# Neighbouring expert tables: one gathered 8 KB row for each pick instead of two of 4 KB, with weights in pairs

## The chip, the cores and the metric

The kernel runs on one core of a Trainium2 chip. The metric is device time in microseconds from start to end of one execution; the median of several is compared. The engines are TensorE (PE, matrix products into PSUM), VectorE (DVE), ScalarE (ACT), GpSimd (POOL, here almost only the issuer of indirect DMAs) and SyncE (SP, the issuer of all other DMAs). Each engine runs its own instructions in program order and waits on semaphores.

## The reference, cut to what matters

Two transformer blocks on 256 tokens of width 1024, all in float32. The first has neighbourhood attention, a convolution and a 16-expert feed-forward layer. The second has differential attention with a spatial gating branch and then, as its feed-forward layer, PEER: for each token and each of 8 heads 16 of 16384 experts are picked, and each expert is one row of `u_tab` and one of `v_tab`.

```python
def peer(h, w_query, sub_keys, u_tab, v_tab):
    xt = h.reshape(T, D)                                   # T = 256, D = 1024
    q = rmsnorm((xt @ w_query).reshape(T, PEER_HEADS, 2, PEER_PK_DIM))
    s = jnp.einsum('thpd,pnd->thpn', q, sub_keys).astype(jnp.float32)
    s1, i1 = lax.top_k(s[:, :, 0], PEER_TOPK)
    s2, i2 = lax.top_k(s[:, :, 1], PEER_TOPK)
    ...
    best, pos = lax.top_k(cand, PEER_TOPK)
    eidx = jnp.take_along_axis(cidx, pos, axis=-1)
    gate = jax.nn.softmax(best, axis=-1)

    def one(args):
        xb, ib, gb = args
        act = jax.nn.gelu(jnp.einsum('td,thkd->thk', xb, u_tab[ib]), approximate=False) * gb.astype(xb.dtype)
        return jnp.einsum('thk,thkd->td', act, v_tab[ib])
```

The lookup moves 256 x 8 x 16 rows of 4 KB from each table, 268 MB in all, against 527 MB for everything else.

## The kernel before, in words

The tokens stand on the 128 partitions in two halves, a = 0 and 1. `work` lists the 16 pairs (half, head); its index is `ix`. For each `ix` there are 16 picks k = 0 to 15, so a pick has the number n = 16 ix + k, 0 to 255. One pick handles one expert for each of the 128 tokens.

A pick goes through these steps:

- Routing: `rt0` to `rt4` (scores on TensorE, top 16 and indices `EI[:, ix, :]` on VectorE, roots and exponentials on ScalarE). GpSimd's gathers of `ix` wait for its indices (event `ei`).
- u: GpSimd gathers 128 rows of `peer_u_2` into a 4 KB buffer (in each partition), line 1636; VectorE takes the dot with the token's vector `HB`, line 1304, into `DOT[:, ix, k]`. The u buffer is then free.
- Weights, once for each `ix` after k = 15: GELU on ScalarE (line 1595), then on VectorE the product with the gate (`weights`, line 1312), which gives `WT`.
- v: GpSimd gathers 128 rows of `peer_v_2`; ScalarE writes `ident` scaled by the weight of each token into one of 4 diagonals `DI` (line 1602); TensorE multiplies diagonal and row, two instructions of `v_step` (line 790) that run as four matmuls of 128x512, and accumulates in two PSUM banks through all 128 picks of a half. The v buffer is free when the matmuls are done.

The order of all of it is one list, `ORDER`, made by `mixer_order`; each engine goes through it and does what is its own. In the PEER part the list has u(ix, k) and v(ix-1, k) side by side, so v is 16 picks behind u. Mixed in are the routing steps of the next `ix`, one at each odd k, and what is left of the second block's mixer for the other half and its queries (`late`, one item at each n that is a multiple of 3). `more_a` and `more_q` are no work: they mark where attention buffers and query weights are done with, and so where the row buffers get more room. `more_a` stands after n = 72 and `more_q` after n = 144, before as after the change. `take` gives the banks of a half to the sums, `leave` ends a half (norm, gain, residual, store).

`row_places` gives the buffers in rotation: 8 for u while ix = 0; then, from `share` on, 4 for u and 4 for v; 6 and 6 from `more_a` on, 10 and 10 from `more_q` on. A gather waits until the last user of its buffer is done.

Weights come by SyncE in blocks of 2 MB; in the PEER part these are `w_branch_attn` and `w_out` (stages `ba`, `op`) and `peer_w_query` (`qm`).

## Time and profile before

| | us |
|---|---|
| median of 3 executions | 2317.37 |
| lowest and highest | 2315.95, 2331.9 |
| the profiled execution, its own time | 2325.88 |
| its span, first to last instruction | 2323.9 |
| busy in the span: TensorE, VectorE, GpSimd, ScalarE | 1756.5, 740.3, 567.2, 392.1 |
| mean granted TensorE clock | 0.893 of full |
| DMA bytes and mean rate | 796.88 MB, 343 GB/s |

The times of single instructions come from the one profiled execution. Its span has 40 slices of 58 us in the strips of the page. GpSimd's first gather starts at 1526.75 us, and its last at 2300.51 us; so the lookup takes the last third of the time, and its first half runs beside the rest of the mixer. DMA share is the mean busy share of 16 DMA engines; it can show 1.00 at quite different GB/s.

### The profile page before, as it was taken

Reading aid. Unit: us, or ns where it says so; the run is one execution under the profiler, and the core shown is the slowest. Engines: PE = TensorE matmul, PEld = TensorE weight load, DVE = VectorE, ACT = ScalarE, POOL = GpSimd, SP = SyncE. Lnnn points to the kernel's source line nnn. Section 1 sums busy time; section 2 is a strip of 40 time slices with the busy share of each in tenths; the row PEclk is TensorE's granted clock in tenths of the full one; section 3 lists DMA queues with packets and bytes.
Section 4 is the critical chain, followed back from the end, with each engine's and each line's share of the span. In section 5 each row is a group of like instructions: output and inputs, shape, how many; then the busy total and the mean of one; then the engine's idle time right before and its main releaser. Section 6 shows DMA issues by size and latency. Waiting matters only on the chain.

```text
span 2323.9 us, 18524 instructions
## 1 busy us (share of the span) xinstructions
PE 1756.5 (76%) x7200; PEld 764.3 (33%) x7200; DVE 740.3 (32%) x1869; ACT 392.1 (17%) x836; POOL 567.2 (24%) x521
## 2 busy tenths in 40 slices
PE   8999656776765566666669999767778888766677
PEld 7656111331211111111124454463333445322223
DVE  5723001000000000000032131366675764766552
ACT  1411010000000000000011442233322222222211
POOL 0000000000000000000000000047676666777774
PEclk9987888887888878787789999889999999999999
DMA  9647999999999999999954332569999999999997
GB/s 370 215 172 298 413 427 427 423 424 424 424 428 428 428 428 428 428 427 428 427 191 160 134 138 79 190 238 365 320 379 388 405 373 359 375 369 369 355 373 292
DMA packets 159334, 796.88 MB, mean 343 GB/s; under 512 B 12304, under 2 KB 12432, under 8 KB 134160
## 3 DMA queue, kind: packets, MB, share of 16 engines
q1 hardware_dynamic: 85520, 527.24, 55.7%
q0 software_dynamic: 73728, 268.47, 30.6%
q8 instruction: 58, 0.95, 0.2%
q14 instruction: 28, 0.23, 0.0%
HBM read 794.61 MB, written 1.05 MB: 342 GB/s over the span
## 4 chain that ended last, share of the span: by engine, by line
PE 40%; DMA 40%; DVE 7%; POOL 7%; ACT 3%; issue 3%; DVEq 0%; POOLq 0%; ACTq 0%
DMA AR<-in_w_down 18%; DMA AR<-in_w_up 15%; PE PS L373 13%; PE PS L790 10%; POOL AR L1636 7%; DMA AR<-in_peer_v,AR 6%; PE PS L594 3%; PE PS L753 2%; PE PS L612 2%; PE PS L384 2%; PE PS L486 1%; DVE AR L856 1%; DMA AR<-in_peer_u,AR 1%; DVE AR L858 1%; PE PS L624 1%
## 5 line engine op out<-in xcount | busy, mean ns | idle before, releaser
L1636 POOL DMA_INDIRECT AR<-in_peer_u,AR x256 | 282.7, 1104 | 1458.4 <-DVE AR L1295 1357.5
L790 PE MATMUL PS<-AR 128*128 128x512 f32 x1024 | 506.9, 635 | 162.2 <-DMA AR<-in_peer_v,AR 93.3
L594 PE MATMUL PS<-AR 128*32 128x512 f32 x2048 | 310.4, 743 | 191.1 <-DMA AR<-in_w_up 127.0
L1304 DVE CUSTOM_DVE_ANT_0 AR<-AR 128x1024 f32<-128x1024 f32 x256 | 308.4, 1221 | 172.8 <-DMA AR<-in_peer_u,AR 172.8
L790 PEld LDWEIGHTS PS<-AR 128*128 128x128 f32 x1024 | 190.3, 199 | 451.2 <-issue 314.0
L373 PE MATMUL PS<-AR 128*128 128x512 f32 x736 | 327.5, 600 | 8.7 <-DVE AR L831 7.9
L1636 POOL DMA_INDIRECT AR<-in_peer_v,AR x256 | 282.7, 1104 | 108.3 <-PE PS L790 56.0
L612 PE MATMUL PS<-AR 128*32 128x512 f32 x1024 | 172.1, 807 | 108.5 <-DMA AR<-in_w_down 99.7
L1035 DVE TENSOR_TENSOR AR<-AR,PS 128x512 f32<-128x512 f32 x16 | 11.0, 688 | 609.5 <-PE PS L594 609.5
L594 PEld LDWEIGHTS PS<-AR 128*32 128x32 f32 x2048 | 63.8, 123 | 424.9 <-DMA AR<-in_w_up 204.4
L373 PEld LDWEIGHTS PS<-AR 128*128 128x128 f32 x736 | 139.2, 193 | 176.1 <-issue 173.1
L1602 ACT ACTIVATE AR<-PK,AR 128x128 f32<-128x128 f32 x256 | 90.7, 393 | 155.0 <-PE PS L790 144.0
L612 PEld LDWEIGHTS PS<-AR 128*32 128x32 f32 x1024 | 32.5, 130 | 231.4 <-DMA AR<-in_w_down 156.9
L1043 DVE COPY AR<-PS 128x512 f32<-128x512 f32 x16 | 11.1, 691 | 286.0 <-PE PS L612 286.0
L384 PE MATMUL PS<-AR 128*128 128x256 f32 x384 | 83.4, 379 | 0.9 <-DVE AR L826 0.9
L624 PE MATMUL PS<-AR 128*128 128x512 f32 x128 | 66.3, 665 | 14.4 <-DVE AR L1043 14.4
L384 PEld LDWEIGHTS PS<-AR 128*128 128x128 f32 x384 | 72.9, 190 | 12.0 <-issue 2.2
L1444 ACT ACTIVATE AR<-PS 128x512 f32<-128x512 f32 x16 | 9.6, 597 | 398.0 <-PE PS L594 398.0
L753 PE MATMUL PS<-AR 128*128 128x128 f32 x512 | 65.6, 291 | 2.1 <-DVE AR L831 2.1
L753 PEld LDWEIGHTS PS<-AR 128*128 128x128 f32 x512 | 64.0, 206 | 4.8 <-DVE AR L826 2.5
L1448 ACT COPY AR<-PS 128x512 f32<-128x512 f32 x16 | 9.4, 585 | 319.9 <-PE PS L601 319.9
L624 PEld LDWEIGHTS PS<-AR 128*128 128x128 f32 x128 | 25.9, 213 | 62.1 <-issue 62.1
(251 smaller groups left out, 1209.3 us busy)
## 6 DMA issues: line engine op xcount, KB each, us to landing
AR<-in_w_gate SPq DMA_DIRECT2D x64, 2048.0 KB, 26.2
AR<-in_w_up SPq DMA_DIRECT2D x64, 2048.0 KB, 25.8
AR<-in_w_down SPq DMA_DIRECT2D x64, 2048.0 KB, 26.4
AR<-in_w_in SPq DMA_DIRECT2D x23, 2048.0 KB, 10.1
AR<-in_w_ada SPq DMA_DIRECT2D x12, 2048.0 KB, 10.0
AR<-in_peer_w_query SPq DMA_DIRECT2D x8, 2048.0 KB, 17.3
AR<-in_w_out SPq DMA_DIRECT2D x6, 2048.0 KB, 13.3
AR<-in_w_branch_attn SPq DMA_DIRECT2D x4, 2048.0 KB, 10.5
```

The costliest lines, as they stand in the source:

```text
L373: i = pe.matmul(PS[:, b, :], src[:, j, a * 128:(a + 1) * 128], IN[key][:, j, :], start=(j == 0), stop=(j == 7))
L384: i = pe.matmul(PS[:, b, q * 256:(q + 1) * 256], IN[key][:, j, (e + q) * 128:(e + q + 1) * 128], src[:, j, :], start=(j == 0), stop=(j == 7))
L486: x = pe.matmul(PS[:, b, :], MT[:, 4 * q + j, a * 128:(a + 1) * 128], IN[key][:, j, n * 512:(n + 1) * 512], start=(j == 0), stop=(j == 3))
L594: x = pe.matmul(PS[32 * q:32 * q + 32, bk, :], XS[:, j, e * 32:(e + 1) * 32], IN[key][:, jj, q * 512:(q + 1) * 512], start=(j == 0), stop= ...
L612: x = pe.matmul(PS[32 * g:32 * g + 32, b, :], HDT[:, s, fq * 32:(fq + 1) * 32], IN[key][:, s, dc * 512:(dc + 1) * 512], start=(fq == 0 and ...
L624: x = pe.matmul(PS[:, y, :], GE[:, r, dc, a * 128:(a + 1) * 128], EO[:, r, :], start=(e == 0), stop=(e == 15), skip_group_check=True)
L753: x = pe.matmul(PS[:, b, q * 128:(q + 1) * 128], IN[key][:, j, (2 * r + q) * 128:(2 * r + q + 1) * 128], HT[:, j, a * 128:(a + 1) * 128], ...
L790: x = pe.matmul(PS[:, ACC[a][m], :], DI[:, n % 4, :], AR[:, off + m * 512:off + (m + 1) * 512], start=(h == 0 and k == 0), stop=(h == 7 an ...
L856: w.step(v.scalar_tensor_tensor(DW[:, j, :], UP[:, j, k:k + 256], c, DW[:, j, :], MULT, ADD))
L1304: v.tensor_tensor_reduce(rows, rows, HB[:, a, :], 1.0, 0.0, MULT, ADD, DOT[:, ix, k:k + 1]).then_inc(*w.hit("dot", ix, k))
L1602: act.activation(DI[:, n % 4, :], ident, ACT.Copy, scale=WT[:, ix, k:k + 1]).then_inc(*w.hit("diag", n))
L1636: pool.indirect_dma_start(out=AR[:, off:off + 1024], out_offset=None, in_=D["peer_u_2" if key == "u" else "peer_v_2"], in_offset=bass.Indi ...
```

## The change

The host puts the two tables side by side, `peer_uv_2` with rows of 8 KB, u first. One gather for each pick brings both, into a buffer of 8 KB for each partition: 128 pieces of 8 KB instead of 256 of 4 KB. The dot reads the first half, the matmuls the second, and the buffer is free when the matmuls are done.

The order list has one loop over n. After row n, for even n, come the weights of the pair (n-2, n-1) and the v steps of these two; GELU of a pair stands after its odd row. So v is 2 picks behind u instead of 16, and GELU (ScalarE) and the product with the gate (VectorE) are 128 instructions each on 2 columns instead of 16 on 16 columns. The buffers are 4 of 8 KB, 7 from `more_a` on (one more place is used, at `W0 + 2048`), 11 from `more_q` on.

```diff
--- before.py
+++ after.py
@@ -294,26 +294,25 @@
                 todo += x
             todo += [("rt1", 0), ("rt2", 0), ("rt3", 0), ("rt4", 0)]
             routes = []
-            for ix in range(17):
-                if ix == 1:
-                    todo.append(("share",))
-                if ix == 8:
+            for n in range(257):
+                ix, k = divmod(n, 16)
+                if n == 128:
                     todo.append(("take", 1))
-                for k in range(16):
-                    if ix < 16:
-                        todo.append(("u", ix, k))
-                    if ix >= 1:
-                        todo.append(("v", ix - 1, k))
-                    if (16 * ix + k) % 3 == 0 and late:
-                        todo += late.pop(0)
-                    if k == 0 and ix < 15:
-                        routes += [(f"rt{s}", ix + 1) for s in range(5)]
-                    if (k % 2 or ix == 0) and routes:
-                        todo.append(routes.pop(0))
-                if ix < 16:
-                    todo.append(("wts", ix))
-                if ix in (8, 16):
-                    todo.append(("leave", ix // 8 - 1))
+                if n < 256:
+                    todo.append(("row", ix, k))
+                if n and n % 2 == 0:
+                    todo.append(("wts", *divmod(n // 2 - 1, 8)))
+                    todo += [("v", *divmod(j, 16)) for j in (n - 2, n - 1)]
+                if n in (128, 256):
+                    todo.append(("leave", n // 128 - 1))
+                if n % 3 == 0 and late:
+                    todo += late.pop(0)
+                if k == 0 and ix < 15:
+                    routes += [(f"rt{s}", ix + 1) for s in range(5)]
+                if (k % 2 or ix == 0) and routes:
+                    todo.append(routes.pop(0))
+                if k % 2:
+                    todo.append(("gelu", ix, k // 2))
             assert not late and not routes
             return todo
 
@@ -321,28 +320,29 @@
         ROWS = {}
 
         def row_places():
             def slot(i):
-                return [NARENA + i * SLOT + 1024 * k for k in range(4)]
-
-            bufs, n = {"u": slot(4) + slot(5), "v": []}, {"u": 0, "v": 0}
-            free = {x: ("used", "wq", 1, 0) if x >= NARENA + 5 * SLOT else ("used", "wq", 0, 0) for x in bufs["u"]}
-            for u, *x in ORDER:
-                if u == "share":
-                    bufs["v"], bufs["u"], n["u"] = bufs["u"][4:], bufs["u"][:4], 0
-                if u in ("more_a", "more_q"):
-                    new = {"u": [o + 16384, o + 18944], "v": [o + 17408, o + 19968]} if u == "more_a" else {"u": slot(2), "v": slot(3)}
-                    for key in "uv":
-                        bufs[key] += new[key]
-                        for k in new[key]:
-                            free[k] = ("mm", "av", 15) if u == "more_a" else ("used", "wq", 2 if key == "u" else 3, 1)
-                if u in ("u", "v"):
-                    k = bufs[u][n[u] % len(bufs[u])]
-                    n[u] = (n[u] + 1) % len(bufs[u])
-                    ROWS[(u, *x)] = k, free[k]
-                    free[k] = ("dot", *x) if u == "u" else ("mm", "row", *x)
+                return [NARENA + i * SLOT, NARENA + i * SLOT + 2048]
+
+            bufs, n = slot(4) + slot(5), 0
+            free = {k: ("used", "wq", i // 2, 0) for i, k in enumerate(bufs)}
+            for stage, *x in ORDER:
+                if stage == "more_a":
+                    new = [o + 16384, o + 18944, W0 + 2048]
+                    free.update({k: ("mm", "av", 15) for k in new})
+                    bufs = bufs[:n] + new + bufs[n:]
+                if stage == "more_q":
+                    new = slot(2) + slot(3)
+                    free.update({k: ("used", "wq", 2 + i // 2, 1) for i, k in enumerate(new)})
+                    bufs = bufs[:n] + new + bufs[n:]
+                if stage == "row":
+                    k = bufs[n]
+                    n = (n + 1) % len(bufs)
+                    ROWS[(*x,)] = k, free[k]
+                    free[k] = ("mm", "row", *x)
 
         row_places()
 
@@ -783,11 +783,11 @@
             def v_step(ix, k):
                 a, h = work[ix]
                 n = 16 * ix + k
-                off, _ = ROWS["v", ix, k]
+                off, _ = ROWS[ix, k]
                 w.wait_ge("diag", n)
-                w.wait_ge("rowv", ix, k)
+                w.wait_ge("landed", ix, k)
                 for m in range(2):
-                    x = pe.matmul(PS[:, ACC[a][m], :], DI[:, n % 4, :], AR[:, off + m * 512:off + (m + 1) * 512],
+                    x = pe.matmul(PS[:, ACC[a][m], :], DI[:, n % 4, :], AR[:, off + 1024 + m * 512:off + 1024 + (m + 1) * 512],
                                   start=(h == 0 and k == 0), stop=(h == 7 and k == 15), skip_group_check=True)
                 x.then_inc(*w.hit("mm", "row", ix, k))
 
@@ -1295,21 +1295,22 @@
                 v.tensor_copy(EI[:, ix, :], EF[:, 0:16]).then_inc(*w.hit("ei", ix))
                 v.tensor_scalar(SMX[:, ix, 0:1], BV[:, ix, 0:1], -1.0, None, MULT).then_inc(*w.hit("smx", ix))
 
-            def u_step(ix, k):
+            def row(ix, k):
                 a, h = work[ix]
-                off, _ = ROWS["u", ix, k]
+                off, _ = ROWS[ix, k]
                 rows = AR[:, off:off + 1024]
-                w.wait_ge("rowu", ix, k)
+                w.wait_ge("landed", ix, k)
                 w.wait_ge("hb", a, 1)
                 v.tensor_tensor_reduce(rows, rows, HB[:, a, :], 1.0, 0.0, MULT, ADD, DOT[:, ix, k:k + 1]).then_inc(*w.hit("dot", ix, k))
 
-            def weights(ix):
-                sm = SMX[:, ix, :]
-                w.wait_ge("gate", ix)
-                w.step(v.reciprocal(sm[:, 1:2], sm[:, 1:2]))
-                w.wait_ge("gelu", ix)
-                w.wait_step()
-                v.scalar_tensor_tensor(WT[:, ix, :], GT[:, ix, :], sm[:, 1:2], WT[:, ix, :], MULT, MULT).then_inc(*w.hit("wt", ix))
+            def weights(ix, p):
+                sm, two = SMX[:, ix, :], slice(2 * p, 2 * p + 2)
+                if p == 0:
+                    w.wait_ge("gate", ix)
+                    w.step(v.reciprocal(sm[:, 1:2], sm[:, 1:2]))
+                    w.wait_step()
+                w.wait_ge("gelu", ix, p)
+                v.scalar_tensor_tensor(WT[:, ix, two], GT[:, ix, two], sm[:, 1:2], WT[:, ix, two], MULT, MULT).then_inc(*w.hit("wt", ix, p))
 
             def leave(a):
                 ps = PS[:, ACC[a][0]:ACC[a][1] + 1, :].rearrange("p b n -> p (b n)")
@@ -1326,7 +1327,7 @@
                     "cmb": att_combine, "gain1": lambda: row_of("g1", G1, COL[:, 3, :]), "gain2": lambda: row_of("g2", G2, COL[:, 4, :]),
                     "hn1": hn1, "hn2": hn2, "ht": heads_turn, "bae": bae, "ope": ope, "up1": up1, "up2": up2, "fn1": fn1, "fn2": fn2,
                     "norm_turn": lambda a: scaled("h3", HT[:, :, a * 128:(a + 1) * 128], a, COL[:, 0, :], COL[:, 5, :]),
-                    "ft": ffn_turn, "rt0": rt0, "rt1": rt1, "rt2": rt2, "rt3": rt3, "rt4": rt4, "u": u_step, "wts": weights, "leave": leave}
+                    "ft": ffn_turn, "rt0": rt0, "rt1": rt1, "rt2": rt2, "rt3": rt3, "rt4": rt4, "row": row, "wts": weights, "leave": leave}
             for stage, *x in ORDER:
                 if stage in mine:
                     mine[stage](*x)
@@ -1590,13 +1591,14 @@
                     act.copy(d[:, 4 * q:4 * q + 4, :], PS[:, banks.at("hb", a, q), :].rearrange("p (j q) -> p j q", j=4)).then_inc(
                         *w.hit("hb", a, q))
 
-            def weights(ix):
-                w.wait_ge("dot", ix, 15)
-                act.activation(WT[:, ix, :], DOT[:, ix, :], ACT.Gelu).then_inc(*w.hit("gelu", ix))
+            def gelu(ix, p):
+                two = slice(2 * p, 2 * p + 2)
+                w.wait_ge("dot", ix, 2 * p + 1)
+                act.activation(WT[:, ix, two], DOT[:, ix, two], ACT.Gelu).then_inc(*w.hit("gelu", ix, p))
 
             def v_step(ix, k):
                 n = 16 * ix + k
-                w.wait_ge("wt", ix)
+                w.wait_ge("wt", ix, k // 2)
                 if n > 3:
                     w.wait_ge("mm", "row", *divmod(n - 4, 16))
                 act.activation(DI[:, n % 4, :], ident, ACT.Copy, scale=WT[:, ix, k:k + 1]).then_inc(*w.hit("diag", n))
@@ -1613,7 +1615,7 @@
                     "hn1": lambda a: root(("on", a), SSO[:, a * 8:a * 8 + 8]), "yt": lambda a: copied("yt", YT, a), "ope": ope,
                     "up1": lambda a: root(("y2", a), ss5[:, a:a + 1]), "up2": up2, "fn1": lambda a: root(("x5", a), ss6[:, a:a + 1]),
                     "qm": qm, "qs": qs, "rt0": lambda ix: root(("q", ix), RQ[:, work[ix][0], 2 * work[ix][1]:2 * work[ix][1] + 2]),
-                    "rt4": rt4, "back": back, "wts": weights, "v": v_step, "leave": leave}
+                    "rt4": rt4, "back": back, "gelu": gelu, "v": v_step, "leave": leave}
             for stage, *x in ORDER:
                 if stage in mine:
                     mine[stage](*x)
@@ -1629,17 +1631,17 @@
             w.step(pool.memset(msk[0:64, 0:1], 1.0))
             pool.memset(msk[64:128, 1:2], 1.0).then_inc(*w.hit("msk"))
 
-            def gather(key, ix, k):
-                off, free = ROWS[key, ix, k]
+            def row(ix, k):
+                off, free = ROWS[ix, k]
                 w.wait_ge("ei", ix)
                 w.wait_ge(*free)
-                pool.indirect_dma_start(out=AR[:, off:off + 1024], out_offset=None, in_=D["peer_u_2" if key == "u" else "peer_v_2"],
+                pool.indirect_dma_start(out=AR[:, off:off + 2048], out_offset=None, in_=D["peer_uv_2"],
                                         in_offset=bass.IndirectOffsetOnAxis(ap=EI[:, ix, k:k + 1], axis=0)).then_inc(
-                    *w.hit(f"row{off}", key, ix, k, also=[("row" + key, ix, k)], by=16))
+                    *w.hit(f"row{off}", ix, k, also=[("landed", ix, k)], by=16))
 
             for stage, *x in ORDER:
-                if stage in ("u", "v"):
-                    gather(stage, *x)
+                if stage == "row":
+                    row(*x)
 
 
 
@@ -1834,8 +1836,9 @@
     for n in ("w_gate", "w_up", "w_down"):
         arrays[n] = g[n][0]
     arrays["final_g"] = g["final_g"]
-    for n in ("w_in_2", "w_branch_attn_2", "w_branch_sgu_2", "w_out_2", "peer_w_query_2", "peer_u_2", "peer_v_2", "b_gate_2"):
+    for n in ("w_in_2", "w_branch_attn_2", "w_branch_sgu_2", "w_out_2", "peer_w_query_2", "b_gate_2"):
         arrays[n] = g[n][0]
+    arrays["peer_uv_2"] = np.concatenate([g["peer_u_2"][0], g["peer_v_2"][0]], 1)
     arrays["rows"] = np.stack([g["sgu_ln_g_2"][0], g["sgu_ln_b_2"][0]])
     return {k: np.ascontiguousarray(a) for k, a in arrays.items()}
 
```

## Rows read from the trace of the kernel before

**Rows 1.** The page, part 2: TensorE's clock and DMA share in 40 slices.

```profile
PEclk9987888887888878787789999889999999999999
DMA  9647999999999999999954332569999999999997
```

**Rows 2.** The stages as windows, busy us (instructions), clock, DMA share, GB/s.

```profile
core 0: us, PE busy (x) PEld busy (x) DVE busy (x) ACT busy (x) POOL busy (x), PEclk, DMA share, GB/s
1526.70:1732.00 205.30, 153.19 (x543) 80.62 (x542) 139.58 (x375) 65.78 (x164) 145.18 (x129) 0.90 0.93 343
1732.00:1964.50 232.50, 200.29 (x688) 106.57 (x687) 145.04 (x382) 54.66 (x131) 156.33 (x144) 0.96 1.00 381
1964.50:2287.00 322.50, 233.43 (x497) 87.59 (x495) 199.62 (x505) 72.63 (x167) 252.79 (x229) 0.97 0.98 371
```

**Rows 3.** The timeline of GpSimd (start, duration, both us): u 72 and u 144.

```profile
1731.97 0.94 POOL L1636 DMA_INDIRECT AR<-in_peer_u,AR  x1 [0.30 <-issue]
...
1964.54 0.94 POOL L1636 DMA_INDIRECT AR<-in_peer_u,AR  x1 [0.30 <-issue]
```

**Rows 4.** Two more windows: an expert stretch, and the last gathers.

```profile
700.00:1150.00 450.00, 275.59 (x1557) 60.53 (x1556) 14.18 (x28) 8.88 (x15) 0.00 (x0) 0.80 1.01 428
2261.00:2300.00 39.00, 32.42 (x70) 12.59 (x71) 13.07 (x24) 7.22 (x19) 29.57 (x31) 1.00 1.03 410
```

**Rows 5.** Groups of instructions from 1480 us on (busy us, mean ns | idle before).

```profile
L1636 POOL DMA_INDIRECT AR<-in_peer_u,AR x256 | 282.7, 1104 | 1458.4 <-DVE AR L1295 1357.5 <-issue 74.4 <-DVE AR L1304 26.6
...
L1595 ACT ACT_TABLE_LOAD x15 | 19.2, 1283 | 0.3
```

**Rows 6.** Line 1636, GpSimd's gathers, 1964.5 to 2287: idle before (us, times).

```profile
  issue: 54.3, 178
  PE PS L790: 15.7, 51
```

**Rows 7.** The timeline: GELU, product of weights and the scaled copies after the last dot.

```profile
2287.00 0.21 ACT L1595 ACTIVATE AR<-AR 128x16 f32<-128x16 f32 x1 [7.72 <-DVE AR L1304]
...
2287.25 0.23 DVE L1312 SCALAR_TENSOR_TENSOR AR<-AR 128x16 f32<-128x16 f32 x1 [0.21 <-ACT AR L1595]
2287.52 0.69 ACT L1602 ACTIVATE AR<-PK,AR 128x128 f32<-128x128 f32 x2 [0.30 <-DVE AR L1312]
```

**Rows 8.** The timeline: the first gather, the first dot, a gather among dots.

```profile
1526.75 1.08 POOL L1636 DMA_INDIRECT AR<-in_peer_u,AR  x1 [1357.48 <-DVE AR L1295]
...
1531.27 1.22 DVE L1304 CUSTOM_DVE_ANT_0 AR<-AR 128x1024 f32<-128x1024 f32 x1 [4.74 <-DMA AR<-in_peer_u,AR]
...
1559.93 1.99 POOL L1636 DMA_INDIRECT AR<-in_peer_u,AR  x1 [0.30 <-issue]
```

**Rows 9.** The timeline: scaled copy to matmul, and matmul to gather.

```profile
1661.11 0.98 ACT L1602 ACTIVATE AR<-PK,AR 128x128 f32<-128x128 f32 x3
1661.57 0.30 PEld L790 LDWEIGHTS PS<-AR 128*128 128x128 f32 x2 [0.27 <-ACT AR L1602]
...
2150.62 1.96 PE L790 MATMUL PS<-AR 128*128 128x512 f32 x4 [0.59 <-DMA AR<-in_peer_v,AR]
...
2152.82 1.01 POOL L1636 DMA_INDIRECT AR<-in_peer_v,AR  x1 [0.31 <-PE PS L790]
```

**Rows 10.** The timeline: four matmuls after an idle time.

```profile
1655.45 3.49 PE L790 MATMUL PS<-AR 128*128 128x512 f32 x4 [2.48 <-ACT AR L1602]
```

**Rows 11.** DMA from issue to landing of the gathers, stage A; stage B with its bytes.

```profile
DMA to landing us min/median/max: 4.5/6.4/10.1
...
DMA to landing us min/median/max: 5.0/8.4/13.0
...
DMA packets 27061, 88.50 MB, mean 381 GB/s; under 512 B 2408, under 2 KB 2408, under 8 KB 27049
```

**Rows 12.** The chain that ended last: a block of 16 matmuls.

```profile
1752.91 6.87 PE PS L373 x16
```

**Rows 13.** The timeline: the last matmuls, 17 picks.

```profile
2287.13 29.42 PE L790 MATMUL PS<-AR 128*128 128x512 f32 x68 [0.60 <-DMA AR<-in_peer_v,AR]
```


## The prediction

> **What bounds the kernel now.** I read the 40 slices first [rows 1]: the digits change character in slice 27, where GpSimd begins to work and the DMA share climbs back to 9. That is the expert lookup (PEER), and only there does the change act. Then the same stretch cut at the picks at which the buffers grow [rows 2]. I number the 256 picks n = 16·ix + k. The order list gives `more_a` right after row 72 and `more_q` right after row 144. The gathers of u 72 and u 144 are the 129th and the 273rd on GpSimd's queue, and they start at 1731.97 and 1964.54 us [rows 3]. So there are three stages: A, 1526.7 to 1732 (72 picks, 205 us, few buffers), B, 1732 to 1964.5 (72 picks, 232.5 us), C, from there to the last product at 2316.6 (112 picks).
>
> In stage C the DMA share is 0.98, but at 371 GB/s. That isn't this core's ceiling: the experts' weights ran at 428 GB/s in slices that show 1.01, and the gathers themselves at 410 GB/s at the end of the stage [rows 4]. What sets C is GpSimd's issue. A gather costs 1104 ns there [rows 5], and 0.30 us of idle time "issue" follows it: of 229 gathers 178 waited for nothing else, and for buffers only 15.7 us in all [rows 6]. (1.104 + 0.30) x 2 = 2.81 us a pick, and 114 picks a 322.5 us stage is 2.82. TensorE (233 of 322.5 us), VectorE (200) and ScalarE (73) have room. Stage B is crowded: TensorE 200 of 232.5 us, DMA share 1.00 with w_query and w_out loads beside the rows. Stage A has slack everywhere (TensorE 153, VectorE 140 of 205 us) and still takes about 2.85 us a pick.
>
> **The change, part by part.**
>
> *One gather for two.* It removes 256 instructions of GpSimd, 256 x 1.41 = 361 us of its queue. Stage C then loses its bound. The next one is the transfer: 1.049 MB a pick at 428 GB/s is 2.45 us, at 410 GB/s 2.56 us; I take 2.50, as the 8 KB pieces lie between the 4 KB of the gathers and the longer ones of the weights. TensorE needs 1.96 us a pick at most, VectorE about 200/114 = 1.75. GpSimd's 1.41 is hidden under the transfer; uncovered it would be late only if an issue took over 2.5 us.
>
> *Weights in pairs.* ScalarE gets 112 more GELUs of 0.21 us (24 us), VectorE 112 more products of 0.23 us (26 us) [rows 7]. Also, a GELU now stands between the root and the exponential of a head, so up to 16 more table loads of 1.28 us (20 us) [rows 5]. All lie in time that both engines wait for rows (ScalarE is busy for 66 of 205 us in the fullest stage); only the one product that releases each pair is on a path, and I count it below. Without that cover they would cost 70 us.
>
> *Buffers.* This is the part that decides. Before, a u buffer was free once its dot was done and a v buffer was filled only 16 picks later, shortly before its product. Now one 8 KB buffer is held from the issue until both matmuls are done. There are 4 of them until row 72, 7 until row 144, then 11; before it was 4 + 4, 6 + 6, 10 + 10. And there is a new wait: on VectorE `wts` of the pair (n-2, n-1) is queued behind `row` n, which waits for row n to land. Behind it wait the copies of `ident` scaled by the weights (the diagonals), the matmuls of n-2, and the gather of n+2, which needs that buffer. With 4 buffers this is a closed loop for each two picks, with nothing of it overlapped:
> - gather issued to dot started, 4.52 us for 512 KB on an empty queue [rows 8], plus the other 512 KB, 1.22 us at 428 GB/s: 5.74
> - dot of row n: 1.22, then 0.05 (an estimate; both are on VectorE) to the product of weights, 0.23, and 0.04 to ScalarE [rows 7, 8]: 1.54
> - diagonal started to matmul started: 0.45 (1661.11 to 1661.57) [rows 9]
> - four matmuls 1.96, and 0.24 until GpSimd starts the next gather [rows 9]: 2.20
>
> Together 9.93 us for two picks, where two gathers' worth of issue allowed 5.6. To that I add two terms. The clock: stage A had 0.90 of full clock with TensorE busy for 75%; in the loop it is busy for about half. After 2.5 us of idle time the four matmuls took 3.49 us [rows 10] instead of 1.96, the lower of the two clock levels (1.2 for 2.4 GHz); bounds 0 and 1.53. The expert stage, with TensorE busy for 61%, has a mean of 0.80 [rows 4]; with less work I take half of the turns at the lower level, 0.75. Late mixer work and routing mixed in between: before, 112 gathers from 1559.93 to 1731.97 [rows 3, 8] took 3.07 us a pick where the issue alone gives 2.81, 0.26 a pick or 0.5 a pair; the bounds are 0 and 1.5 (routing instructions on VectorE are short and lie in the 6 us in which it waits for a row). So 11.2 us a pair, with bounds 9.9 and 13.
>
> Row 4 needs the product of row 0, behind the dot of row 2: row 2 lands at 1526.75 + 5.7 + 2 x 2.45 = 1537.4, and 3.95 us of chain and 0.24 of issue later gather 4 goes out at 1541.6. Gather 72 follows 34 pairs later: 1541.6 + 34 x 11.2 = 1922.4, against 1732.0. Stage A costs +190 us.
>
> *A queue effect inside the loop.* GpSimd's gathers take 0.94 us when VectorE is not in a dot, and up to 1.99 when dots run back to back, as at 1559.93 [rows 8]. Gather n+2 goes out when the dots are over, so I take 0.94 (it is inside the 5.74), and 1.05 x 34 = 36 us as the upper end. The Trainium skill, SBUF — State Buffer, Who interferes with whom, says that a VectorE instruction with two SBUF inputs contends with a GpSimd instruction that reads SBUF, and that the second to start waits; the rows above agree, and by it alone the price would be anything from 0 to those 36 us.
>
> *Stage B.* With 7 buffers the same loop turns 5 picks at a time: 9.9/5 = 2.0 us, under the 3.23 a pick that the stage took. TensorE's work and the bytes are what they were, so I leave it at 232.6 us. Lower bound: 88.5 MB [rows 11] at 410 GB/s, 216 us. Upper: one 6.87 us block like those of `op` or `ba` [rows 12] in each turn, 18.1/5 = 3.6 a pick, 260 us. Gather 144 at 2155.0.
>
> *Stage C.* 11 buffers give 9 picks a turn, 1.1 us: the transfers rule. Row 144 lands some 9 us after its issue (8.4 us was the median for 512 KB in the crowded stage) [rows 11], at 2164. Then 111 x 2.50 = 277.5: row 255 lands at 2441.5. The indices of the next head are ready after dot 16·ix + 9 and 3.5 us of `rt4`, with six rows still in flight, so that isn't late.
>
> *The end.* Before, 68 matmuls of the last 17 picks stood behind the last dot (29.4 us [rows 13]). Now it is dot 1.22, GELU 0.3, product 0.27, diagonal 0.49, two picks 1.96 + 1.72: 6.0 us, to 2447.5, and the same 7.35 us of `leave`, from 2316.6 to the end of the span. Span 2454.9 against 2323.9: +131 us. The profiled execution took 2325.88, 2 us more than its span, and lies 8.5 us over the median; the difference goes on the median: 2317.4 + 131 = 2448.
>
> In brief: stage A +190, stage B 0, stage C and the end -59.
>
> **The rivals.**
> (1) *Faster: the number of transfers is what counts.* If the loop of stage A weren't closed, because rows landed early enough that four buffers cover them, A would stay at 205 us and only the -59 remain: 2258 us. For it: GpSimd's issue is the plain bound in C. Against it: it decides at a loop of 11.2 - 131/34 = 7.35 us, and landing plus dot alone are 6.96. The Trainium skill, DMA: Bandwidth & Descriptors, Bandwidth, asks for transfers of at least 1 MiB; by it this change is right, and the time would be this rival's. The landing of stage A (4.5 us at best, 6.4 in the median [rows 11]) neither proves nor refutes it.
> (2) *The loop is longer.* Late work falls into it, and in stage B too: 13 us a pair (+61) and 3.6 us a pick in B (+27): 2536 us. For it: in-order queues, where a scaled copy waits behind an exponential that waits for VectorE. Against it: 6 us of idle time in each turn.
> (3) *The 8 KB row isn't one piece.* If the gather writes it as two, an issue costs 2 x 0.94 us: +0.94 in each turn (32 us), and the transfer stays at 2.56 us (+7): 2487 us. No row of before has an 8 KB gather.
>
> **How the numbers follow.** My forecast with its own bounds (loop 9.9 to 12.5, B 216 to 245, C 2.45 to 2.6) runs from 2380 to 2515 and gets 0.72; rival 2 0.11, rival 3 0.08, rival 1 0.06, nothing measurable 0.03. The range 2375 to 2530 takes in rival 3 and the near half of rival 2. A difference under 1% can hardly be told from none here. Faster 0.06, same 0.03, slower 0.91.
>
> **What would show it.** Right: GpSimd idle in stage A for some 10 us at every second gather, ended by the matmuls; gathers in pairs; DMA share near half and TensorE's clock below 0.9 until `more_a`; stage A near 395 us; stage C at 2.5 us a pick with TensorE or VectorE waiting for rows; a last block of matmuls of two picks. Wrong: a gather 72 before 1880, a landing of 8 KB rows much under 5.7 us, or stage C still at 2.8 us. It would all fall if the loop had overlap that I missed, above all if VectorE could take a pair's weights ahead of the next row.

## The result, and the profile after

The changed kernel takes 2505.7 us (median of 4, 2502.39 to 2512.94), the kernel before 2322.72 in the same comparison: ratio 1.0785, 95% interval 1.0759 to 1.0811. The profiled execution took 2506.88 us with a span of 2505.1.

Page, part 2, of the changed kernel: clock and DMA share in 40 slices of 63 us.

```profile
PEclk9988878888888778877999998777777889999999
DMA  9657999999999999998443246555555988899997
```

In slices 25 to 31 the DMA share stays at 5 and 6, where the kernel before was at 9 from its slice 28 on [rows 1], and in slices 26 to 31 the clock is at 7. From slice 32 on the DMA share is at 8 and 9. The same in windows, cut where GpSimd issues the first gather and rows 72 and 144 (columns as in rows 2):

```profile
core 0: us, PE busy (x) PEld busy (x) DVE busy (x) ACT busy (x) POOL busy (x), PEclk, DMA share, GB/s
1528.60:1937.10 408.50, 235.45 (x612) 113.98 (x612) 153.95 (x428) 97.28 (x224) 68.68 (x72) 0.77 0.54 195
1937.10:2206.10 269.00, 207.53 (x653) 107.82 (x652) 144.10 (x394) 73.96 (x173) 78.32 (x73) 0.90 0.86 326
2206.10:2473.00 266.90, 214.93 (x486) 90.85 (x486) 193.92 (x533) 83.81 (x208) 130.70 (x111) 0.94 1.01 421
```

| stage (start of issue to start of issue, us) | before | forecast | after |
|---|---|---|---|
| first gather | 1526.8 | 1526.8 | 1528.6 |
| A, to row 72 | 205.2 | 395.6 | 408.5 |
| B, to row 144 | 232.6 | 232.6 | 268.9 |
| C with the end, to the end of the span | 359.4 | 299.9 | 299.0 |

The loss is in A (+203) and B (+36); C with the end gives back 60. The next lines are those of line 1638, GpSimd's gathers in stage A of the changed kernel: number and durations; the idle time before them by what ended it (us, times); who waited for them (us, times); and the time from issue to landing.

```profile
L1638 POOL DMA_INDIRECT AR<-in_peer_uv,AR x72: 933/936/1375, 1528.6 to 1928.2; - x72
...
  PE PS L790: 330.3, 68
...
  DVE AR L1304: 226.6, 66
...
DMA to landing us min/median/max: 5.3/5.7/9.7
```

GpSimd stood 330 of 408 us at a matmul, 68 of 72 times, and VectorE 227 us at a landing. Neither is overlapped with the other, as one turn of the loop shows (timeline of the changed kernel: start, duration, both us):

```profile
1800.40 0.94 POOL L1638 DMA_INDIRECT AR<-in_peer_uv,AR  x1 [8.29 <-PE PS L790]
...
1806.53 1.23 DVE L1304 CUSTOM_DVE_ANT_0 AR<-AR 128x1024 f32<-128x1024 f32 x1 [8.32 <-DMA AR<-in_peer_uv,AR]
...
1807.68 0.22 DVE L1313 SCALAR_TENSOR_TENSOR AR<-AR 128x2 f32<-128x2 f32 x1
1807.93 0.69 ACT L1604 ACTIVATE AR<-PK,AR 128x128 f32<-128x128 f32 x2 [9.49 <-DVE AR L1313]
...
1808.38 6.45 PE L790 MATMUL PS<-AR 128*128 128x512 f32 x8 [6.65 <-ACT AR L1604]
...
1812.44 0.94 POOL L1638 DMA_INDIRECT AR<-in_peer_uv,AR  x1 [9.49 <-PE PS L790]
```

The gather of an even row goes out at 1800.40 (that of the odd row 1.6 us behind it isn't shown). The dot starts 6.13 us later, the pair's weights come right behind the dot, then the scaled copies and the first four matmuls, and at 1812.44 the next gather: 12.04 us for two picks. The mean turn from gather 4 to gather 72 is (1937.15 - 1548.44)/34 = 11.43 us.

Two groups of the page, for comparison with rows 5 (busy us, mean ns | idle before):

```profile
L1638 POOL DMA_INDIRECT AR<-in_peer_uv,AR x256 | 278.6, 1088 | 2024.0 <-DVE AR L1295 1385.7
...
L1597 ACT ACT_TABLE_LOAD x37 | 47.5, 1283 | 0.7
```

A gather of 8 KB rows costs GpSimd what one of 4 KB did (1088 against 1104 ns), and there are 37 table loads at GELU's line instead of 15. The roots and exponentials beside it also load more often; in this part of the kernel there are 80 loads in all where there were 52. At the end of the kernel the last block of matmuls is four picks, not 17 [rows 13]:

```profile
2490.63 7.13 PE L790 MATMUL PS<-AR 128*128 128x512 f32 x16 [1.25 <-ACT AR L1604]
```

### The profile page after: what moved, and what is told of

The parts are those of the page before. It is cut to its first block, busy times and chain, and to the rows that moved or that the text cites. A ratio compares the mean times of both kernels' runs of the same rounds, so it can differ in the third digit from the quotient of the medians.

```text
span 2505.1 us, 18590 instructions
## 1 busy us (share of the span) xinstructions
PE 1825.0 (73%) x7200; PEld 799.6 (32%) x7200; DVE 758.4 (30%) x1981; ACT 452.0 (18%) x976; POOL 280.4 (11%) x265
## 3 DMA queue, kind: packets, MB, share of 16 engines
HBM read 794.61 MB, written 1.05 MB: 318 GB/s over the span
## 4 chain that ended last, share of the span: by engine, by line
DMA 43%; PE 40%; DVE 10%; ACT 4%; issue 2%; POOL 1%; DVEq 0%; POOLq 0%; ACTq 0%
DMA AR<-in_w_down 16%; DMA AR<-in_w_up 14%; DMA AR<-in_peer_uv,AR 13%; PE PS L373 12%; PE PS L790 12%; DVE AR L1304 3%; PE PS L594 2%; PE PS L753 2%; PE PS L612 2%; PE PS L384 2%; PE PS L486 1%; DVE AR L856 1%; ACT AR L1604 1%; DVE AR L858 1%; PE PS L624 1%
## 5 line engine op out<-in xcount | busy, mean ns | idle before, releaser
L790 PE MATMUL PS<-AR 128*128 128x512 f32 x1024 | 571.7, 714 | 290.5 <-ACT AR L1604 290.4
L1638 POOL DMA_INDIRECT AR<-in_peer_uv,AR x256 | 278.6, 1088 | 2024.0 <-DVE AR L1295 1385.7
L790 PEld LDWEIGHTS PS<-AR 128*128 128x128 f32 x1024 | 225.6, 229 | 607.8 <-ACT AR L1604 348.6
L373 PE MATMUL PS<-AR 128*128 128x512 f32 x736 | 327.3, 600 | 8.7 <-DVE AR L831 7.9
L373 PEld LDWEIGHTS PS<-AR 128*128 128x128 f32 x736 | 139.0, 192 | 176.0 <-issue 173.1
L624 PE MATMUL PS<-AR 128*128 128x512 f32 x128 | 68.4, 683 | 14.4 <-DVE AR L1043 14.4
L384 PEld LDWEIGHTS PS<-AR 128*128 128x128 f32 x384 | 74.4, 194 | 12.6 <-issue 2.2
L753 PEld LDWEIGHTS PS<-AR 128*128 128x128 f32 x512 | 61.4, 199 | 5.6 <-issue 3.1
L1313 DVE SCALAR_TENSOR_TENSOR AR<-AR 128x2 f32<-128x2 f32 x128 | 28.0, 218 | 66.2 <-ACT AR L1597 65.9
L1597 ACT ACT_TABLE_LOAD x37 | 47.5, 1283 | 0.7
```

The lines of the kernel that those rows point to most:

```text
L373: i = pe.matmul(PS[:, b, :], src[:, j, a * 128:(a + 1) * 128], IN[key][:, j, :], start=(j == 0), stop=(j == 7))
L384: i = pe.matmul(PS[:, b, q * 256:(q + 1) * 256], IN[key][:, j, (e + q) * 128:(e + q + 1) * 128], src[:, j, :], start=(j == 0), stop=(j == 7))
L624: x = pe.matmul(PS[:, y, :], GE[:, r, dc, a * 128:(a + 1) * 128], EO[:, r, :], start=(e == 0), stop=(e == 15), skip_group_check=True)
L753: x = pe.matmul(PS[:, b, q * 128:(q + 1) * 128], IN[key][:, j, (2 * r + q) * 128:(2 * r + q + 1) * 128], HT[:, j, a * 128:(a + 1) * 128], ...
L790: x = pe.matmul(PS[:, ACC[a][m], :], DI[:, n % 4, :], AR[:, off + 1024 + m * 512:off + 1024 + (m + 1) * 512], start=(h == 0 and k == 0), s ...
L1313: v.scalar_tensor_tensor(WT[:, ix, two], GT[:, ix, two], sm[:, 1:2], WT[:, ix, two], MULT, MULT).then_inc(*w.hit("wt", ix, p))
```

## The experiments

The times of both kernels and of e1, e2, e5 and e9 are medians, those of the other runs single executions. Beside each stands the kernel before on the same chip. The first two lines of the table are the two kernels.

Stages A and B run to the issue of row (or u) 72 and 144, in one profiled execution of each run. Where two kernels do the same work, these stages agree closely: A is 329.8 in e1 and 331.5 us in e6, and 408.5 in the changed kernel and 408.6 in e3. Only B of the kernel before (232.6) and of e9 (227.7) are 5 us apart, so differences under some 5 us say little.

| run | edit | time, before beside it (us) | A | B |
|---|---|---|---|---|
| before | | 2322.7 | 205 | 233 |
| changed | | 2505.7, 2322.7 | 408.5 | 269 |
| e1 | changed, weights ahead of row | 2427.9, 2324.6 | 330 | 271 |
| e2 | changed, two tables | 2438.2, 2324.6 | 306 | 271 |
| e3 | changed, 4 buffers in B too | 2663.9, 2324.6 | 408.6 | 427 |
| e4 | changed, extra matmuls in A | 2507.4, 2324.6 | 403 | 270 |
| e5 | before, weights in pairs | 2339.6, 2318.0 | 210 | 239 |
| e6 | e1, v one step later | 2418.3, 2318.0 | 331.5 | 260 |
| e7 | e1, copy for GELU | 2394.4, 2318.0 | 309 | 258 |
| e8 | e5 with v 2 behind u | 2355.0, 2322.7 | 238 | 252.5 |
| e10 | e5 with v 6 behind u | 2365.8, 2322.7 | 232 | 257 |
| e11 | e8, v gathered with u | 2434.4, 2316.6 | 307.5 | 275 |
| e9 | before to row 143, then joined | 2296.6, 2318.0 | 206 | 228 |

Theory 1 was the closed loop of the prediction: with four buffers each turn holds two picks, and nothing in it overlaps. Its rivals: theory 2, slow 8 KB gathers; theory 3, the pairs with their table loads; theory 4, stage B bound by late work; and theory 5, formed after the first four runs, the short lag of v (2 picks behind u, not 16).

**e1, the queue place of the weights.**

```diff
-                if n < 256:
-                    todo.append(("row", ix, k))
                 if n and n % 2 == 0:
                     todo.append(("wts", *divmod(n // 2 - 1, 8)))
+                if n < 256:
+                    todo.append(("row", ix, k))
+                if n and n % 2 == 0:
                     todo += [("v", *divmod(j, 16)) for j in (n - 2, n - 1)]
```

> VectorE takes the weights of the pair (n-2, n-1) ahead of row n instead of behind it; everything else as changed. Theory 1 (the loop of stage A is closed by that queue place: landing of row n, dot, weights, diagonal, matmuls, next gather, for two picks): the loop then spans four picks: second gather 2.2 us after the first, landing 5.7, dot 1.2, GELU 0.3, weights and diagonal 0.75, matmuls 2.0 to 3.5, 0.24, so 12.2 to 13.7 us for four picks; stage A falls from 408 to 220 to 250 us, stage B from 269 to 235 to 260, the total to 2320 to 2360. Theory 2 (8 KB gathers into four buffers are slow whatever the order: landing and clock): stage A stays over 380 us and the total over 2470.

Measured: ratio to before 1.0453 (1.0423 to 1.0482); stages A and B of e1 in windows:

```profile
1523.30:1853.10 329.80, 202.56 (x613) 102.44 (x612) 154.47 (x428) 97.62 (x224) 75.04 (x73) 0.81 0.65 242
1853.10:2124.50 271.40, 205.54 (x653) 106.85 (x652) 143.44 (x391) 74.11 (x173) 76.63 (x73) 0.89 0.85 324
```

One list entry moved gives back 79 of the 203 us of stage A, so the place of `wts` behind `row` is a cause, and theory 2, as it was put, falls. But both are far outside what I expected: stage A is 80 us above the top of its range, the total 68, and B didn't move. Something takes the place of the wait that was removed. A part of it is VectorE's wait for GELU. The group of the product of a pair's weights in stage A, first in the changed kernel and then in e1 (busy us, mean ns | idle before):

```profile
L1313 DVE SCALAR_TENSOR_TENSOR AR<-AR 128x2 f32<-128x2 f32 x35 | 7.6, 217 | 1.1 <-ACT AR L1597 1.0
...
L1314 DVE SCALAR_TENSOR_TENSOR AR<-AR 128x2 f32<-128x2 f32 x35 | 7.7, 221 | 39.1 <-ACT AR L1598 39.1
```

Behind the dot of row n the GELU had long been done; ahead of it VectorE stands 39 us for ScalarE, with the dot of row n queued behind.

**e2, two tables.** Orders, pairs and buffer places are those of the changed kernel, but u and v are gathered by themselves, v right behind u on GpSimd, and u's half of the buffer is free after its dot.

```diff
-                w.wait_ge(*free)
-                pool.indirect_dma_start(out=AR[:, off:off + 2048], ..., in_=D["peer_uv_2"],
+                for key, at, free in (("u", off, free_u), ("v", off + 1024, free_v)):
+                    w.wait_ge(*free)
+                    pool.indirect_dma_start(out=AR[:, at:at + 1024], ..., in_=D["peer_u_2" if key == "u" else "peer_v_2"],
```

> Weights in pairs and v two picks behind u as changed, but two tables and two 4 KB gathers for each pick, u's buffer free after its dot, as many buffers of each as the changed kernel has of 8 KB. Theory 1 (u and v held together is half of the closed loop): the gather of u n no longer waits for matmuls of pick n-4 except through GpSimd's queue; M(n-4) to M(n) is three issues 3.96, landing 5.5, dot 1.2, 0.8, matmuls 2.0 to 3.5, so 13.5 to 15 us for four picks, stage A 240 to 270 us; stage C goes back to GpSimd's 2.8 us a pick (315 us); total 2340 to 2390. Theory 3 (the pairs with their table loads and the short lag cost by themselves): stage A stays near 400 us and the total is over 2500.

Measured: ratio 1.05 (1.0468 to 1.0531), stage A 306.4, B 271.0. Joining the rows, with all else equal, makes 2505.7 us of 2438.2: it costs 102 us in A and gives back 28 in C with the end (299.0 against 326.6). From row 144 to the last issue it gives back 42 (266.9 against 308.6), but 14 of these are lost again, as with the joined rows the end takes 32 us from the last issue and with two tables 18. Theory 3 alone doesn't hold, and theory 1 missed too: 306 is above its 240 to 270, and the total above its 2340 to 2390.

**e3, four buffers in stage B.**

```diff
                 if stage == "more_a":
                     ...
-                    bufs = bufs[:n] + new + bufs[n:]
+                    held = new
```

> The three buffers of more_a come into use only at more_q, so that four buffers last to row 144. Theory 1 (4-buffer loop of 11.4 us for two picks): stage B turns at the pace of stage A, 72 x 5.7 = 410 us against 269, total about 2645. Theory 4 (stage B is bound by TensorE's late blocks and the weights' loads, not by the loop): stage B under 320 us, total under 2560.

Stage B of e3, in a window:

```profile
1935.70:2362.30 426.60, 263.48 (x698) 129.96 (x697) 152.25 (x403) 76.67 (x183) 67.91 (x72) 0.79 0.57 208
```

Stage B takes 426.6 us, 5.9 a pick and 4% over theory 1's 410, with DMA at 0.57. So the number of buffers sets the pace, also where TensorE has its large late blocks. Theory 4's bound is refuted for four buffers.

**e4, the clock.**

```diff
+                if k % 2 and n < 72:
+                    w.wait_ge(*banks.last.get(7, ()))
+                    for _ in range(3):
+                        pe.matmul(PS[:, 7, :], ident, HB[:, 0, 0:512], start=True, stop=True, skip_group_check=True)
```

> After each pair of v steps of stage A TensorE also multiplies three 128x512 blocks into a bank that nothing reads (that bank is taken out of the rotation until row 128); the output is unchanged. Theory 1 with the clock term (matmuls of the loop run at the lower clock level, 876 ns mean each, and cost it about 1.5 us a turn): the granted clock in stage A rises from 0.77 to over 0.9, the mean of line 790 falls under 700 ns, stage A falls by 25 to 50 us to 360 to 385, total 2455 to 2480. Rival: the matmuls are not in the loop or the added ones delay as much as they give; stage A 400 to 440 us.

Matmul groups of stage A (1532.6 to 1935.5), e4 first, line 796 being the added ones, and then the changed kernel:

```profile
L790 PE MATMUL PS<-AR 128*128 128x512 f32 x277 | 173.7, 785 | 102.4 <-ACT AR L1608 102.4
L796 PE MATMUL PS<-AR,PK 128*128 128x512 f32 x204 | 93.1, 592 | 0.0
```

```profile
L790 PE MATMUL PS<-AR 128*128 128x512 f32 x275 | 195.5, 876 | 172.0 <-ACT AR L1604 172.0
```

The clock of the stage rose from 0.77 to 0.87 and the mean of the v matmuls fell from 876 to 785 ns, neither as far as expected, and the stage fell only by 5.6 us instead of 25 to 50; at 402.9 us it is in the rival's range. The timelines, turn by turn (means over the 34 turns from gather 4 to gather 72), say why. From the first v matmul to the next gather a turn takes 3.15 us instead of 3.81, so the better clock gives back 0.66, or 22 us in the stage. But from dot to matmul it takes 2.27 instead of 1.91, nearly all of it in four turns of 3.7 to 6.0 us, and from gather to dot 5.84 instead of 5.71. In the turn of 5.66 us a late block of 32 matmuls (line 753) that ScalarE waits for had to stand behind the added ones. So this much of better clock is worth some 22 us of the 203, and the added matmuls take most of it back. At the upper level in every turn (2.25 us, as in nine turns of e4) it would be 53 us, an estimate.

**e5, pairs alone.** The kernel before, with only the GELU and the product of weights in pairs:

```diff
                         todo.append(("u", ix, k))
+                    n = 16 * ix + k
+                    if n and n % 2 == 0 and n <= 256:
+                        todo.append(("wts", *divmod(n // 2 - 1, 8)))
...
-                if ix < 16:
-                    todo.append(("wts", ix))
+                    if k % 2 and ix < 16:
+                        todo.append(("gelu", ix, k // 2))
```

> The kernel before (two tables, v 16 picks behind u, its own buffers) with one part of the change: GELU and weights for each pair right after its dots. Theory 5 (what is left of the loss, stage B above all, is the lag of two picks: each pair of matmuls waits in line behind a dot, a GELU and the routing and mixer steps between them): the pairs cost nothing when v stays 16 behind; stages 205, 232 and 336 us as before, total 2310 to 2335. Theory 3 (the pairs with their table loads cost by themselves): stage B 250 to 270, total 2360 or more.

Measured: ratio 1.0102 (1.008 to 1.0123), 2339.6 us, a little above theory 5's range of 2310 to 2335 and under theory 3's 2360: the pairs cost 21 us by themselves. Stages A and B:

```profile
1528.50:1738.70 210.20, 155.14 (x542) 82.70 (x541) 144.03 (x406) 89.29 (x209) 139.65 (x129) 0.89 0.91 335
1738.70:1977.80 239.10, 195.30 (x652) 102.56 (x650) 145.64 (x408) 69.19 (x169) 153.60 (x145) 0.96 0.97 369
```

**e6 and e7, what closes the shorter loop.** Both on top of e1. e6:

```diff
+                if n > 73 and n % 2 and n != 129:
+                    todo += [("v", *divmod(j, 16)) for j in (n - 3, n - 2)]
```

> Weights first, and from more_a on the two v steps of a pair stand one pick later on all engines (at the odd step, ahead of the next GELU). Theory 5: with a diagonal ready earlier TensorE waits less for ScalarE; stage B falls from 271 to 240 to 258 us, total 2400 to 2415. Rival (stage B is bound by the seven buffers, which the later matmuls hold longer): stage B 275 us or more.

e7 replaces GELU by a copy, so it leaves out a part of the computation:

```diff
-                act.activation(WT[:, ix, two], DOT[:, ix, two], ACT.Gelu)...
+                act.activation(WT[:, ix, two], DOT[:, ix, two], ACT.Copy)...
```

> Weights first, and a plain copy in the place of GELU, so that no table is loaded for it (part of the computation is left out). If the table loads stand in the short chain from dot to matmul, stage A falls from 330 by 14 x 1.3 = 18 us or more and stage B from 271 by some 14; if they are hidden under the waits for rows, both stay within 5 us.

Stage B of e6, then stages A and B of e7:

```profile
1855.50:2115.80 260.30, 205.01 (x683) 109.77 (x682) 145.77 (x396) 75.18 (x178) 77.77 (x72) 0.92 0.88 337
```

```profile
1526.30:1835.30 309.00, 199.57 (x612) 100.95 (x612) 151.66 (x419) 70.62 (x203) 77.75 (x72) 0.85 0.69 258
1835.30:2093.80 258.50, 204.73 (x653) 106.28 (x652) 146.86 (x400) 56.63 (x161) 75.42 (x73) 0.91 0.89 340
```

e6 takes 11 us off stage B (271.4 to 260.3), where 13 to 31 were expected; its total, 2418.3, is just above its range, since stages A and C are each 2 us longer than in e1. e7 takes 20.8 us off A and 13.0 off B. Without GELU between them the roots and exponentials load fewer tables too: stage A has 10 loads where e1 has 30, stage B 9 where it has 22, and at 1.28 us each that is 25.7 and 16.7 us of ScalarE's time. So some four fifths of that time had been on the path. In the kernel before one GELU served the matmuls of 16 picks; here every pair has its own, and its matmuls follow at once. VectorE's wait for GELU in stage A falls from 39 to 22 us. What else keeps stage A of e1 at 330 us, and e7's at 309, stays open. The Trainium skill, ScalarE: Activation LUTs, Table sets: the hidden batching unit, asks to batch activations by set; by that rule the pairs with a root and an exponential between them were the wrong direction, and both stages of e7 agree (20.8 and 13.0 us).

**e8, e10 and e11, the lag and GpSimd's queue.** e8 and e10 are e5 with the list written for any lag, v 2 or 6 picks behind u. In e8 the lines that set it are:

```diff
-            for ix in range(17):
...
+            for n in range(256 + 2):
...
+                if n >= 2:
+                    todo.append(("v", *divmod(n - 2, 16)))
```

> The kernel of the run with pairs at lag 16 (two tables, separate buffers 4, 6, 10 of each), but v only 2 picks behind u; nothing else differs. Theory 5 (the short lag costs by itself): stage A 280 to 310 us against 210, stage B 262 to 275 against 239, total 2420 to 2450. Rival (only joined buffers make the lag expensive, since u is held): stage A under 240, total under 2370.

> The same with v 6 picks behind u. Theory 5 in the form that the lag must cover one late step with its round trips (some 10 us, 3 to 4 picks): most comes back, stage A 210 to 235 us, stage B 236 to 250, total 2335 to 2370. If the cost grew evenly with each pick less of lag, stage A would be near 280 and the total near 2400.

e8 measured A 238.2, B 252.5, total 2355.0, in the range of the rival. e10 measured 232.0, 257.3 and 2365.8: A and the total are in their ranges, B is not, and lag 6 is no better than lag 2. So theory 5 falls as the main cause. From lag 16 to 2 the total grows by about 11 us, net of the runs beside them; as these are single executions, and those of the kernel before spread over 16 us, that is hardly more than a sign. The stages show more: A grows by 28 us and B by 13, and C with the end shrinks by 24 (358.7 to 334.5). A part of this is work that moves: with the short lag GpSimd has 70 v gathers to issue in stage A, not 56, and 14 issues at 1.41 us would be 20 of the 28 us, an estimate. e11 then changes one thing in e8:

```diff
-                if stage in ("u", "v"):
-                    gather(stage, *x)
+                if stage == "u":
+                    gather("u", *x)
+                    gather("v", *x)
```

> The kernel of the run with two tables and lag 2, with one edit on GpSimd: the gather of v n stands right behind that of u n instead of two picks later. Same transfers, buffers and orders on the other engines. Theory 1 (what costs is that a pick's v row is asked for, and its buffer held, before u n+1 and n+2 can be asked for, so that GpSimd's queue stands at a matmul): stage A rises from 238 to 290 to 310 us, total 2355 to 2420-2440. Rival (the two-table runs differ by v in pairs and by buffer counts): stage A stays under 250, total under 2370.

GpSimd's gathers in stage A, one line of the idle time before them (who ended it: us, times) and one of who waited for them, e8:

```profile
  PE PS L792: 32.9, 22
...
  DVE AR L1306: 38.8, 25
```

and e11:

```profile
  PE PS L792: 116.6, 35
...
  DVE AR L1306: 125.3, 47
```

The total rises from 2355.0 to 2434.4 us and stage A from 238 to 307.5, both as theory 1 expected. Same bytes, same buffers, same work: when v is asked for together with u, it needs a free v buffer two picks earlier, GpSimd stands at the matmuls that free one for 117 instead of 33 us, and the next u, queued behind, comes late (125 instead of 39 us of waiting on VectorE).

**e9, a version from what was learned.** The kernel before up to row 143; then, when the mixer is done and there is room, the joined table in 7 and soon 11 buffers of 8 KB, pairs, weights first. The 16 picks whose v is still missing are caught up four at a time.

```diff
+            for n in range(144, 257):
+                ...
+                if n > 144 and n % 2 == 0:
+                    todo.append(("wts", *divmod(n // 2 - 1, 8)))
+                if n < 256:
+                    todo.append(("row", ix, k))
+                end = min(j + 4, n - n % 2)
+                if n % 2 == 0 or n < 148:
+                    todo += [("v", *divmod(i, 16)) for i in range(j, end)]
```

> The kernel before up to row 143, then the joined table with weights in pairs and v two picks behind, in 7 and then 11 buffers of 8 KB, when no mixer work is left. Theory 1 and 5 together: stages A and B stay at 205 and 232 us, and the rest moves 126 MB at 420 GB/s instead of two issues of 1.4 us a pick, 300 us, with 13 us of end: total 2265 to 2290, faster than both kernels. If the joined rows themselves were slow, it would be over 2320.

Measured: 2296.6 us, ratio 0.9917 (0.9896 to 0.9938): 0.8% faster than the kernel before, and above my 2265 to 2290. Stages A, B and C in windows, and C's rate in 40 slices:

```profile
1526.20:1732.10 205.90, 151.34 (x546) 80.99 (x545) 139.37 (x375) 65.93 (x165) 143.44 (x128) 0.91 0.93 342
1732.10:1959.80 227.70, 196.07 (x678) 104.87 (x677) 145.11 (x383) 54.55 (x131) 156.51 (x145) 0.97 1.00 387
1959.80:2258.80 299.00, 240.95 (x529) 101.85 (x528) 194.67 (x532) 91.35 (x224) 148.44 (x127) 0.94 0.99 403
```

```profile
GB/s 361 343 259 348 412 202 313 410 426 422 422 423 420 421 419 422 422 422 422 423 419 421 422 422 422 422 421 422 421 420 421 422 420 423 422 422 420 421 422 422
```

A and B are those of before. C takes 299 us from the issue of row 144 to the last issue and ends 33.3 us later, 332 in all against 359. The slices (7.5 us each) show what is missing: six of the first eight, where v is caught up, move 202 to 361 GB/s. After that it is mostly 420 to 422.

## Why the prediction was right, and where it wasn't

The direction, the place and the mechanism in stage A were right, and the range held the time, near its upper end; the point was 58 us low. 50 of these are in the span (14.8 until gather 72, of which 1.9 lie ahead of the first gather, then 36.3 in B and -0.9 in C), and 7 in the step from the profiled execution to the median: it lay 8.5 us over the median before and 1.2 after.

- *The loop of stage A.* 11.43 us a turn against 11.2. Its terms, as means over the 34 turns: gather to dot 5.71, forecast 5.74; dot to matmul 1.91, forecast 1.99; four matmuls with the issue 3.81, forecast 2.20 plus 0.75 for the clock. So the clock term was too small: 1.61 instead of 0.75, just over my upper bound of 1.53, as 22 of the 34 turns, not half of them, took over 4 us for this part (the mean v matmul of the stage took 876 ns, where the added ones of e4 show 592). And the 0.5 for late work didn't show: the first two terms came out 0.1 shorter than forecast. The two errors cancel for the most part; that the turn was hit within 0.25 us is in part luck. The turns make 8 us of the stage's 14.8; the rest is the start: gather 4 at 1548.4, not 1541.6. e1, e3 and e11 show that the loop is real. But the queue place of the weights, which the prediction names as what closes it, is worth 79 of the 203 us; with it gone the stage still takes 330.
- *The queue effect on GpSimd* (up to 36 us) didn't come: its gathers in stage A took 936 ns in the median and 1375 at most.
- *Stage B: the step that failed.* "The same loop turns 5 picks at a time: ... so I leave it at 232.6 us." It took 268.9, above my upper bound of 260. The loop alone doesn't explain it, since opening it (e1) changed nothing. What the runs show in it are v asked for together with u (23 us, e11 against e8), the lag of 2 (13 us, e8 against e5), table loads on the path (13 us, e7), the place of the v steps (11 us, e6), and the pairs (6.5 us, e5). I had taken each resource's total and not the chain dot, GELU, weights, copy, matmul, which late steps of three engines now interrupt. These overlap and don't add up as they stand; the table at the end of this section has steps that do.
- *The pairs at no cost.* Partly wrong. Without any short lag they cost 21 us (e5), and there were 28 more table loads (22 at GELU's line), where I had bounded them by 16. The cover I named, waits for rows, is gone as soon as the row isn't what is waited for.
- *Stage C and the end.* Right: 299.0 us against 299.9, at 421 GB/s, and rows landed in 17.2 us in the median since the queue was full. The last block was one of four picks (7.13 us), not of two (3.7).
- *The rivals.* The faster one (2258 us) is refuted: landing plus dot alone, 5.7 + 1.2 us, filled most of a turn, and DMA stood at 0.54. The third is refuted, an issue cost the same for 8 KB. The second had its pace in B about right (3.7 us a pick against 3.6), but not in A.

Step by step from the kernel before to the changed one, the stages of the profiled executions change so (us; C with the end):

| step | A | B | C |
|---|---|---|---|
| weights in pairs (e5) | +5 | +6.5 | -1 |
| v 2 instead of 16 behind u (e8) | +28 | +13 | -24 |
| v asked for with u (e11) | +69 | +23 | -9 |
| v in pairs, places of the changed kernel (e2) | -1 | -4 | +1 |
| rows joined (changed) | +102 | -2 | -28 |

In total times, each against the run of before beside it, the steps are +21, +11, +86, -4 and +69 (single executions for e8 and e11). The order of the steps is one choice; others would share the loss out differently.

## What to carry to other kernels

Two transfers of which one is wanted later are not two halves of one transfer: joining them makes the buffer of both live from the first issue to the last use, so work out buffers divided by (landing + all until release) before counting saved issues. In in-order queues look at what stands ahead of the instruction that releases a buffer; here one list entry was worth 79 us. Against two tables in the same order, joining cost 102 us with four buffers, made no clear difference with seven (2 us), and gave back 28 with eleven, where the issue had been the bound.

## What the runs showed of the hardware

- A gather of 128 rows of 8 KB takes GpSimd as long as one of 4 KB (median 936 against 940 ns), and lands in 5.3 us at best against 4.5 [rows 11]; so by these best cases the second 512 KB cost about 0.8 us, less than the 1.22 that the rate of rows 4 would give.
- Gathers of 8 KB rows ran at 420 to 422 GB/s for some 200 us, those of 4 KB rows, which the issue limits, at 371 over stage C [rows 2] and 410 at best [rows 4].
- In stage A of the changed kernel TensorE was busy for 58% of the time, and the granted clock was 0.77; in the turn shown, eight matmuls that began after 6.65 us of idle time took 6.45 us, where other blocks of eight, at the upper level, took 3.70 at a granted clock of 1.00 (e4 at 1756.97 us, the changed kernel at 2470.76). With the added matmuls of e4 it was busy for 74%, and the clock was 0.87.
- A table load took ScalarE 1283 ns each time. Of the 20 loads (25.7 us) that fell away in stage A of e7, 20.8 us came back in the stage's time, and of 13 (16.7 us) in stage B 13.0.
